# A one-core transformer kernel whose modulation vectors are multiplied and summed by GpSimd, with TensorE left to add over the partitions

## The reference, cut to what matters

```python
def first_block(x, c, positions, mod_w, mod_b, norm1_g, norm2_g, ...):
    for l in range(DEPTH):
        mod = c @ mod_w[l] + mod_b[l]
        sh1, sc1, g1, sh2, sc2, g2 = [m[:, None, :] for m in jnp.split(mod, 6, axis=-1)]
        h = _rmsnorm(x, norm1_g[l]) * (1.0 + sc1) + sh1
        x = x + g1 * _mixer(h, positions, w_in[l], forget_bias[l], w_branch_a[l], w_branch_b[l], w_out[l])
        h = _rmsnorm(x, norm2_g[l]) * (1.0 + sc2) + sh2
        x = x + g2 * _conv_ffn(h, w_up[l], conv_w[l], conv_b[l], w_down[l])
    return _rmsnorm(x, final_g)
```

## Time and profile before

| what | value |
|---|---|
| median of 3 runs | 1545.51 us (1545.39 to 1545.8) |
| profiled execution, its own time | 1546.15 us |
| span of the profiled execution | 1544.3 us |
| mean granted TensorE clock | 0.991 of 2.4 GHz |
| busy: PE, DVE, ACT, POOL | 97%, 74%, 54%, 3% |

### The profile page before, as it was taken

How to read it: one execution, slowest core, us unless ns; L and a number is a source line. 1 busy time by engine, 2 the same in 40 slices (tenths; PEclk the granted TensorE clock), 3 DMA queues, 4 the chain that set the end, 5 groups by cost and what they waited for, 6 DMA issues and landing times.

```text
span 1544.3 us, 31324 instructions
## 1 busy us (share of the span) xinstructions
PE 1496.4 (97%) x12608; PEld 1435.3 (93%) x12608; DVE 1145.4 (74%) x2186; ACT 832.3 (54%) x1509; POOL 52.2 (3%) x60
## 2 busy tenths in 40 slices
PE   5999999999999999999999999999999999999997
PEld 3898898999998999989999989999999999999997
DVE  4757666888646577759997678878966888888774
ACT  3655544655435646447555555645455754645453
POOL 1000002000000000010001000000000200000000
PEclk8999999999999999999999999999999999999998
DMA  9655565576776452454555543443446444444430
GB/s 395 247 199 189 197 234 195 206 278 253 272 270 261 173 201 87 155 200 164 178 180 193 218 164 112 171 183 137 155 153 243 144 158 161 167 164 140 167 131 28
DMA packets 47839, 290.50 MB, mean 188 GB/s; under 512 B 9992, under 2 KB 12296, under 8 KB 13136
## 3 DMA queue, kind: packets, MB, share of 16 engines
q1 hardware_dynamic: 38880, 280.83, 48.9%
q10 hardware_dynamic: 8816, 7.67, 1.5%
HBM read 286.09 MB, written 2.39 MB: 187 GB/s over the span
## 4 chain that ended last, share of the span: by engine, by line
PE 55%; DVE 2%; ACT 1%; issue 1%; POOL 0%; DVEq 0%; POOLq 0%; ACTq 0%
PE bank L1351 16%; PE bank L1357 16%; PE bank L1352 16%; PE bank L1601 2%; PE sums L1526 1%; PE sums L1416 1%; PE bank L1390 1%; PE bank L1395 1%; PE bank L1389 1%; PE bank L1508 1%; PE bank L1499 1%; DVE macc L2047 0%; DVE w_lo L2042 0%; ACT w_hi L1649 0%; DVE x L2047 0%
## 5 line engine op out<-in xcount | busy, mean ns | idle before, releaser
L1351 PE MATMUL bank<-h_hi,w_hi 128*128 128x256 f32 x2256 | 634.0, 288 | 8.9 <-ACT h_hi L1746 3.7
L1352 PE MATMUL bank<-h_hi,w_lo 128*128 128x256 f32 x2256 | 623.5, 284 | 0.0
L2042 DVE TENSOR_TENSOR w_lo<-ring,w_hi 128x1024 fp32r<-128x1024 f32 x436 | 524.0, 1223 | 104.9 <-ACT w_hi L1649 102.2
L1357 PE MATMUL bank<-h_lo,w_hi 128*128 128x256 f32 x2256 | 577.0, 284 | 0.2 <-DVE h_lo L2047 0.2
L1649 ACT ACTIVATE w_hi<-ring 128x1024 fp32r<-128x1024 f32 x436 | 449.1, 1054 | 131.8 <-PE bank L1357 131.2
L1351 PEld LDWEIGHTS bank<-h_hi,w_hi 128*128 128x128 f32 x2256 | 433.8, 192 | 22.7 <-issue 17.7
L1352 PEld LDWEIGHTS bank<-h_hi,w_lo 128*128 128x128 f32 x2256 | 434.2, 192 | 0.6 <-issue 0.5
L1357 PEld LDWEIGHTS bank<-h_lo,w_hi 128*128 128x128 f32 x2256 | 406.2, 192 | 0.4 <-DVE h_lo L2047 0.4
L1351 PE MATMUL bank<-a_hi,w_hi 128*128 128x256 f32 x352 | 99.7, 283 | 0.3 <-DVE a_lo L2047 0.3
L1352 PE MATMUL bank<-a_hi,w_lo 128*128 128x256 f32 x352 | 98.3, 279 | 0.0
L1357 PE MATMUL bank<-a_lo,w_hi 128*128 128x256 f32 x352 | 98.2, 279 | 0.0
(11 more groups left out here) (344 smaller groups left out, 2371.0 us busy)
## 6 DMA issues: line engine op xcount, KB each, us to landing
ring<-weights SPq DMA_DIRECT2D x266, 1024.0 KB, 4.9
pos_bias<-scratch ACTq DMA_DIRECT2D x4, 512.0 KB, 5.6
x<-x_t ACTq DMA_DIRECT2D x1, 1024.0 KB, 6.6
scratch<-line ACTq DMA_DIRECT2D x1, 1024.0 KB, 4.9
mem_x<-mem_t ACTq DMA_DIRECT2D x1, 1024.0 KB, 5.5
mem_second<-mem_t ACTq DMA_DIRECT2D x1, 1024.0 KB, 6.2
out_t<-x SPq DMA_DIRECT2D x2, 512.0 KB, 2.6
co<-const SPq DMA_DIRECT2D x1, 462.0 KB, 6.9
```

The source lines that it names most:

```text
L1351: pe.matmul(to, WH[:, b % SPLIT, o, :], hi[:, k, :], start=(i == 0), stop=False)
L1352: pe.matmul(to, WL[:, b % SPLIT, o, :], hi[:, k, :], start=False, stop=False)
L1357: last = pe.matmul(to, WH[:, b % SPLIT, o, :], lo[:, k, :], start=False, stop=(i == n - 1))
L2042: ve.tensor_tensor(WL[:, b % SPLIT], ring_half(b), WH[:, b % SPLIT].bitcast(F32), ALU.subtract).then_inc(w_lo_v, 1)
```

## The change

**Who multiplies.** 28 of the 40 later mod chunks go to GpSimd (`eng="gpsimd"`): it multiplies the whole chunk by `c` in place (128 x 2048), adds halves to halves in the ring (128 x 1024, then 128 x 512), and writes the last sum to `modacc` (128 x 256). Each of the four waits for the one before. 12 chunks stay with TensorE as before: those of `gap_mod` and those after the down tiles 2 to 7.

**Who adds over the partitions.** All 40 chunks get a new step `modrow`, at the next mod point after their `mod` step: one fp32 matmul of ones (32 columns) against `modacc` (line 1441 of the changed kernel), then an ACT copy of the result, and after part 3 a DRAM write of one row instead of four. `modload` and `modsum` follow one mod point later than before and handle one row; DVE's two additions of rows go.

**New waits.** TensorE waits in `modrow` for `mod_by_gpsimd`. SP waits for `mod_by_gpsimd` before it reuses the slot. GpSimd, before each chunk, waits until the rows of the vector before are written (`mod_row_out`); for part 0 that is the `modrow` of part 3, which stands at the same mod point.

```diff
+        for st, n in state["rows"]:
+            p.add("modrow", ps=p.full_bank(), part=st.part, n=n, v=st.v, after=st.ps)
+            if st.part == 3:
+                state["summed"] = (st.l, st.g)
+        state["rows"].clear()
...
     def gap_mod():
-        if queue and not state["summed"]:
-            mod(*queue.pop(0))
+        if queue and not state["summed"] and not any(st.part == 3 for st, _ in state["rows"]):
+            mod(*queue.pop(0), by_pe=True)
...
             ps = fm("dn", dn[j], j=j, l=l).ps
-            some_mod()
+            some_mod(by_pe=j >= 2)
...
+                    elif mods[c - RING].eng == "gpsimd":
+                        sp.wait_ge(mod_p, mods[c - RING].v + 1)
...
+            def modrow(st):
+                to = claim(st.ps)
+                if st.v is not None:
+                    pe.wait_ge(mod_p, st.v + 1)
+                else:
+                    wait_taken(pe, st.after)
+                pe.matmul(to[0:32, 0:256], ones[:, 0:32], modacc[:, st.part, :], start=True, stop=True).then_inc(ready, 1)
...
+            def modrow(st):
+                wait_ready(act, st.ps)
+                act.activation(modacc[0:32, st.part, :], bank[st.ps.bank][0:32, 0:256], ACT.Copy).then_inc(
+                    taken[st.ps.bank], 1)
+                if st.part == 3:
+                    wait_taken(act, st.ps)
+                    act.dma_start(mod_rows.ap()[st.n], modacc[0:1, :, :]).then_inc(mod_row_out, 16)
...
+            def mod(st):
...
+                if st.n:
+                    po.wait_ge(mod_row_out, 16 * st.n)
+                wait_loaded(po, st.chunk)
+                w = ring[st.chunk % RING][:].rearrange("p (k c) -> p k c", c=256)
+                to = modacc[:, st.part, :]
+                step(po.tensor_tensor(w, w, ss("c", 0, KD)[:, :, None].broadcast_to([P, KD, 256]), ALU.mult))
+                step(po.tensor_tensor(w[:, 0:4, :], w[:, 0:4, :], w[:, 4:8, :], ALU.add))
+                step(po.tensor_tensor(w[:, 0:2, :], w[:, 0:2, :], w[:, 2:4, :], ALU.add))
+                po.tensor_tensor(to, w[:, 0, :], w[:, 1, :], ALU.add).then_inc(mod_p, 1)
```

More of the change, by code:

```diff
@@ L1699, in mod @@
                     taken[st.ps.bank], 1)
-                if st.part == 3 and st.n is not None:
-                    for u in st.after:
-                        wait_taken(act, u)
-                    act.dma_start(mod_rows.ap()[st.n], modacc[0:97:32, :, :]).then_inc(mod_row_out, 16)
+            def modrow(st):
[5 more added lines that the diff above has]
+                    act.dma_start(mod_rows.ap()[st.n], modacc[0:1, :, :]).then_inc(mod_row_out, 16)
             def modload(st):
```

51 lines of the change are left out of this document (27 added, 24 removed).

## The result

The changed kernel takes 1655.94 us (median of 4 runs, 1652.78 to 1659.52), the kernel before 1545.48 us beside it. The ratio is 1.0717, with a 95% interval of 1.0704 to 1.0730: 110 us slower. The forecast was 1632 us with a range of 1573 to 1670. The direction and the lock between VectorE and GpSimd were right.

The account below looks back on a forecast made before the run. TensorE, busy 97% of the span, was taken as the bound. Up product 56, attention 22, the rest 4 + 4 + 1 gave +87 us on the profiled 1546.15: 1633, so 1632 us at the median; range 1573 to 1670.

Parts of the forecast that it names:

- the lock: VectorE and GpSimd instructions with two SBUF inputs run one after the other, whole; carried from 0.7 us to 5 us.
- What TensorE gives back: On TensorE, 28 moved chunks give 0.57 us each, 12 staying cost 0.43 us more each: net gain 10.8 us.
- The chunk on GpSimd: GpSimd's four instructions for one chunk: 7.9 to 9.8 us, 9.0 taken, 9.4 us with gaps.
- The up product: Layer 0's up product: period from 12.70 to 18.3 us, eleven chunks; term +56 us, between +30 and +70.
- overlaps some 1.3 us: In the up product, a GpSimd chunk runs beside VectorE's PSUM-input taps for some 1.3 us, giving the 18.3 us period.
- The credit of 6.6 us of lead: In the up product, VectorE's finished w_lo blocks ahead of TensorE cover 6.6 us of delay once.
- The wait for the small write: Part 0 waits for the row write before it: 14 us of attention waits; elsewhere ring slack covers it, counted at nothing.
- The attention stage: Layer 0's attention, eight chunks: 14 us of TensorE waits plus 8 us on VectorE; +22 us, between +10 and +36.
- Rival 3: A waiting TensorE is granted the lower clock in part; a few such stretches give 1670 to 1700 us; chance 0.04.
- The rest: Projections +4, down tiles and layer 1 +4, TensorE's balance outside the stages counted +1; ring counted at nothing.
- Rival 1: GpSimd doesn't hold the inputs for a long instruction's length: 1539 to 1549 us, either side of no change; chance 0.12.
- Rival 2: Inputs shared in pieces or good phases: up period 12.7 to 16 us, attention waits 10, total 1550 to 1587; chance 0.12.

Follow-up runs that it names:

- e1_writes_only: The changed kernel with GpSimd's four reading instructions per chunk replaced by five memsets that only write, same waits and slots: 1583.28 us.
- e7_six_chunks: The kernel before with only six of the 40 chunks on GpSimd, at isolated places, and a modrow only for these: 1572.16 us.
- e3_gate_last: The changed kernel with GpSimd's wait for the previous vector's row moved from ahead of the multiply to ahead of the last add: 1634.62 us.
- e11_all_by_tensor: The changed kernel with all 40 chunks multiplied by TensorE, none by GpSimd, each still with its modrow: 1583.92 us.
- e12_pieces_gate_row: The changed kernel with GpSimd's chunk in 15 short instructions, the small-write wait before the last add, and the last up modrow behind the first down tile: 1608.69 us.

## Why the prediction was right, and where its terms were off

**The lock: right.** The deciding step, that two SBUF inputs on VectorE and a GpSimd instruction that reads run one after the other, whole, holds for instructions of 3.6 us. The kernels that only write and only read separate it from everything else. The rule is a little too narrow: the `tensor_scalar` with one SBUF tile was held too.

The Trainium skill (SBUF — State Buffer, "Who interferes with whom") adds that a GpSimd instruction which only writes does not contend; e1_writes_only agrees (`w_lo` 1225 ns beside 112 fills of 1.82 us).

**What TensorE gives back: a little too much.** The mod chunk is 1.00 us, as priced. The `modrow` takes 0.55 us (365.40 to 365.95 in the changed kernel's timeline) where other matmuls follow, as for 29 of the 40, and about the 0.43 of the earlier trace rows only for the 11 with a chunk or another `modrow` behind them (0.41). So the net is 28.0 - 20.5 = 7.5 us, not 10.8.

**The chunk on GpSimd: at the lower end.** The shortest of each size in the changed kernel are 3.60, 2.36, 1.26 and 0.72 us, 7.94 together; the forecast's lower end was 7.9, and 9.0 was taken. The three adds lie nearly on a line, 0.18 us fixed and 0.54 us for each 256 columns. By it 2048 columns would take 4.5 us and the chunk 8.8 us (an estimate), near what was taken; but the multiply is shorter. What sets it apart is that its second input is one column broadcast over 256; that this is the reason was not tested.

**The up product: mechanism right, too dear by a fifth.** Period 18.3 us forecast, 16.2 measured, at the floor of 16.0. With the hold at 7.94 the floor itself is 7.0 + 8.0 = 15.0, and VectorE's groups tell how near it comes. Groups by line of the changed kernel in 324.6 to 454 us:

```profile
L2062 DVE TENSOR_TENSOR w_lo<-ring,w_hi 128x1024 fp32r<-128x1024 f32 x33 | 60.3, 1866 | 0.0
L2437 DVE SCALAR_TENSOR_TENSOR act_val<-tanh_a,conv_b 128x256 f32<-128x256 f32 x16 | 16.7, 1044 | 0.5
L2067 DVE TENSOR_TENSOR a_lo<-act_val,a_hi 128x256 fp32r<-128x256 f32 x16 | 12.0, 749 | 0.0
L2436 DVE SCALAR_TENSOR_TENSOR tanh_a<-tanh_a,conv_a 128x256 f32<-128x256 f32 x16 | 9.6, 602 | 0.0
```

Above their old lengths (1.22, 0.42, 0.42, 0.42 us) these are 20 + 10 + 5 + 3 = 38 us in eight periods, 4.7 us of delay for a chunk of 8.0. VectorE's 10.6 us of own work, 4.7 of delay and 0.9 idle make the 16.2. The step that failed is "overlaps some 1.3 us": the free taps and GpSimd's own waits cover 3.3 us. The credit of 6.6 us of lead was wrong the other way, as e7_six_chunks showed (1.2 us). From the stage came +32 us up to its last mod point and 14 us in one wait, 46 where 56 was forecast. The two numbers are closer than what they stand for: the 56 were VectorE's delay alone, against 32, and the 14 us were forecast as nothing.

**The wait for the small write: seen in one stage, missed in another.** The prediction worked it out for part 0 in the attention (14 us). In the up product it only said that the ring's slack covers it, and did not look at what stands behind the last chunk: `upend`, the chunk and its `modrow` follow each other with nothing between, and GpSimd could not begin before 466.60. That is the 13.6 us wait; e3_gate_last halves it (6.5 us) and takes another 11 us off the other row waits. The attention stage itself came to +18 us against +22, but by other terms: its waits for GpSimd's rows are 4.4 and 3.3 us, 8 where 14 was forecast, and e11_all_by_tensor loses 8 us in the same stage without any chunk on GpSimd.

**The lower clock: the largest miss.** Rival 3 had the mechanism, at 4%, as "a few such stretches" on top of the forecast. It was no rival but a term of every case: the records show 20 stretches at 1.2 GHz of 3.4 to 13.7 us, 111 us in all against 29 before, and beside nearly each of them stands a wait of TensorE of 2 to 14 us (waits of 2.9, 4.5, 3.4 and 4.5 us end at 324.6, 357.6, 389.3 and 422.3; stretches begin at 324.8, 355.6, 389.7 and 420.4). The busy time that it adds is estimated at 32 us, nearly a third of the 110. It is there, with 14 to 38 us, in every experiment with 13 or more chunks on GpSimd. That a wait is what causes each stretch was not tested by itself; the runs show them rise and fall together, and e12_pieces_gate_row, without long waits in the up product, holds 1.00 there. Not every wait has its stretch: behind those of 2.0 us that end at 346.1 and 410.8 the clock stays full.

**The rest: too small by far.** Forecast +9 for projections, down tiles and layer 1; measured about 12 + 4 + 8 + 13 + 8 = 45, part of it the lower clock. Two things were left out. TensorE's own chunks now also wait for ScalarE's copy at `modrow` (6.7 us at 562.5, 12.4 us for two in e11_all_by_tensor). And beside the projections GpSimd holds VectorE's short additions of `score`, again with two SBUF inputs, which the prediction did not look at:

```profile
626.22 10.11 DVE L2304 SCALAR_TENSOR_TENSOR score<-relu,wis,score 128x256 f32<-128x256 f32 x7
```

The seven took 3.81 us before. TensorE waits 6.4 us for what follows them on VectorE, and 4.2 us at the same place of layer 0 (10.6 us in the list of waits).

**The rivals.** Rival 1 (no long lock) priced a kernel without a lock at 1539 to 1549 us. The kernel e1_writes_only is that one, and takes 1583. So even without the lock the change would have lost, by the waits for results and the clock behind them; the 7% for faster rested on a wrong price. Rival 2's good phase did happen in the up product (16.2 us against its 16), and its total did not, for the same missing terms.

In sum, against the forecast: up product -10 us, attention -4, all other stages +36, with the lower clock's 32 us spread over all of them. The total is only some 20 to 24 us off because errors of both signs met, not because the terms were sharp.

## What to carry to other kernels

GpSimd's idle time is not free where VectorE is near its bound with two SBUF inputs: each microsecond in which GpSimd reads costs VectorE up to one, so ask how much of VectorE's work has an input in PSUM (that part is free) and how far ahead of TensorE it really runs, by following which result each matmul takes, not by counting buffers. When a step turns one engine's work into a chain over three (multiply on one, add on another, copy on a third), cost that step alone: here it was 38 us without any GpSimd work, more than the work saved. And count a TensorE wait above its own length where its clock was full before, since matmuls beside it can run at half speed.

## What the runs showed of the hardware

- A GpSimd `tensor_tensor` in fp32 takes at best 3.60 us for 2048 columns with a broadcast second input, and with two full inputs 2.36 for 1024, 1.26 for 512 and 0.72 for 256; a fill of 2048 columns takes 1.82 us.
- A GpSimd fill leaves a VectorE instruction with two SBUF inputs at its 1.22 us; a reading GpSimd instruction holds it until it ends, up to 4.63 us for one `w_lo`, and all 32 `w_lo` of over 1.5 us end 1.08 or 1.09 us behind such an end.
- A VectorE `tensor_scalar` of 256 columns with one SBUF tile as input took 2.50 us instead of 0.35 beside a reading GpSimd instruction.
- Cutting the GpSimd work into pieces of 256 columns keeps VectorE's delay small (waits of TensorE for `w_lo` at most 1.2 us), at 12.7 us instead of 9.3 for a chunk.
- Stretches at 1.2 GHz stand beside TensorE waits as short as 2 to 3 us, and are 3.4 to 13.7 us long in the changed kernel; some waits of 2.0 us have none.
- An fp32 matmul of 256 columns with a stationary of 32 columns takes 0.55 us until the next tile's matmuls start, and 0.41 us ahead of a chunk's.
